# Prompt rows before the weights, one value accumulation for four samples, and ScalarE with two pages of six key slots, in a decoder step

## The reference

```python
z = x @ w_in                                   # q | k | v | B | C | h
page_sum = jnp.sum(cache_k[layer_idx, page_table], axis=2)   # block means -> top-3 blocks per head
s = einsum(q, k) / 8 - slopes * dist;  p = softmax(s where valid)
attn = einsum(p, v)
mix = concat([attn, B * causal_dwconv(C * h)]) @ w_out
x1 = layer_norm(ALPHA * x + mix)
up = causal_dwconv(x1 @ w_up);  a, g = split(up)
y = layer_norm(ALPHA * x1 + (silu(a) * g) @ w_down)
```

## Time and profile before

| | us |
|---|---|
| median of 3 runs (lowest, highest) | 438.06 (437.49, 438.96) |
| the profiled execution, own time | 437.8 |
| its span, first to last instruction | 436.0 |

### The profile page before, as it was taken

How to read it: one execution, slowest core, us unless ns; L and a number is a source line. 1 busy time by engine, 2 the same in 40 slices (tenths; PEclk the granted TensorE clock), 3 DMA queues, 4 the chain that set the end, 5 groups by cost and what they waited for, 6 DMA issues and landing times.

```text
span 436.0 us, 8237 instructions
## 1 busy us (share of the span) xinstructions
PE 412.7 (95%) x2903; PEld 339.2 (78%) x2903; DVE 294.7 (68%) x382; ACT 181.4 (42%) x694; POOL 110.8 (25%) x133
## 2 busy tenths in 40 slices
PE   4999999999999998999999989999999999999990
PEld 4588887876876774765653479999999999999990
DVE  0498999999799976954541275666776776534437
ACT  1587569644469133112110243554455555233201
POOL 1005334995255152200000717122211220000002
PEclk9999999999999999999999999999999999999997
DMA  8999999899999999999999953665556766676002
GB/s 313 397 359 407 405 407 393 316 404 409 409 359 327 338 404 405 406 405 404 402 405 398 318 196 98 194 191 162 158 169 191 213 181 186 183 211 206 3 2 99
DMA packets 109515, 124.60 MB, mean 286 GB/s; under 512 B 5903, under 2 KB 67048, under 8 KB 109466
## 3 DMA queue, kind: packets, MB, share of 16 engines
q1 hardware_dynamic: 101138, 107.30, 70.2%
q10 hardware_dynamic: 8336, 16.78, 10.2%
HBM read 121.65 MB, written 2.61 MB: 285 GB/s over the span
## 4 chain that ended last, share of the span: by engine, by line
PE 64%; DVE 18%; DMA 5%; issue 5%; SPq 4%; POOL 2%; ACT 1%; DVEq 0%; POOLq 0%; ACTq 0%
PE ps L1821 12%; PE ps L1822 11%; PE ps L1823 11%; PE ps L1714 8%; PE ps L1608 6%; DVE qk L939 6%; DVE T L949 5%; PE ps L1437 4%; PE ps L1632 4%; PE ps L1634 3%; PE ps L1384 3%; SPq L360 2%; DMA wring<-in_cache_v 2%; DMA KV<-in_cache_k 2%; POOL x1l L612 1%
## 5 line engine op out<-in xcount | busy, mean ns | idle before, releaser
L1188 DVE TENSOR_TENSOR wlo<-KV,whi 128x2048 fp32r<-128x2048 f32 (+1 forms) x24 | 61.7, 2571 | 57.5 <-ACT whi L838 29.3
L1437 PE MATMUL ps<-xT,wring 128*128 128x264 f32 x384 | 89.6, 388 | 0.1
L1437 PEld LDWEIGHTS ps<-xT,wring 128*128 128x128 f32 x384 | 71.6, 190 | 13.6 <-issue 1.7
L1821 PE MATMUL ps<-x1h,whi 128*128 128x264 f32 x256 | 73.7, 288 | 0.2
L1822 PE MATMUL ps<-x1l,whi 128*128 128x264 f32 x256 | 72.7, 284 | 0.0
L1823 PE MATMUL ps<-x1h,wlo 128*128 128x264 f32 x256 | 72.6, 284 | 0.0
L939 DVE TENSOR_TENSOR qk<-KV,qk 128x1536 f32<-128x1536 f32 (+1 forms) x32 | 67.0, 2097 | 6.6 <-DMA KV<-in_cache_k 2.7
L669 ACT ACTIVATE qk<-qk 128x64 f32<-128x64 f32 x216 | 51.9, 245 | 29.1 <-POOL qk L560 23.1
L949 DVE TENSOR_REDUCE T<-qk 128x24 f32<-128x1536 f32 (+1 forms) x32 | 58.4, 1827 | 0.0
L1821 PE MATMUL ps<-fh,whi 128*128 128x264 f32 x176 | 50.4, 286 | 0.1
L1822 PE MATMUL ps<-fl,whi 128*128 128x264 f32 x176 | 50.0, 284 | 0.0
(11 more groups left out here) (215 smaller groups left out, 574.0 us busy)
## 6 DMA issues: line engine op xcount, KB each, us to landing
KV<-in_cache_k SPq DMA_DIRECT2D x128, 256.0 KB, 6.2
KV<-in_w_ffn_up SPq DMA_DIRECT2D x32, 512.0 KB, 4.7
KV<-in_cache_v SPq DMA_DIRECT2D x60, 256.0 KB, 7.3
wring<-in_cache_v SPq DMA_DIRECT2D x56, 256.0 KB, 6.4
KV<-in_w_ffn_down SPq DMA_DIRECT2D x8, 1408.0 KB, 6.3
wring<-in_w_in ACTq DMA_DIRECT2D x5, 2048.0 KB, 14.0
zbuf<-in_cache_v SPq DMA_DIRECT2D x12, 256.0 KB, 5.3
zbuf<-in_w_ffn_up SPq DMA_DIRECT2D x3, 1024.0 KB, 10.2
```

The source lines that it names most:

```text
L1188: nc.vector.tensor_tensor(wlo[s][:, 0:n], w2[s][:, 0:n], whi[s][:, 0:n], ALU.subtract).then_inc(s_lo, 1)
L1437: ins = nc.tensor.matmul(ps[:, z_bank(n), 0:R], tile[k], xT[:, k, :], start=k == 0, stop=k == KT - 1)
L1821: nc.tensor.matmul(out, wh[k], xh[k], start=k == 0, stop=False)
```

## The change

**Start.** The prompt rows go to ACT's queue as its first transfer. The first block of `w_in` goes to SP's queue, behind a wait for `ident`, and ahead of the keys. PE's warming products use `ones` in place of `ident`, stand first in its list and number 11. Six of the eight row transposes stand before the q product, two behind it; ACT copies all eight before the first q copy. **Keys.** In the six slots of `HALVED` ACT sums two pages and DVE two; `multiply` two slots later waits for ACT's sums. **Values.** The weights of four samples lie in four buffers (two of them in `ftmp` and in `ct`/`dist`, zeroed by POOL between its key pages), each in its own eight columns, and 16 value slots accumulate in one bank. So `masked_values`, `sample_outputs` and `sample_columns` run twice and not eight times; four products with a new 4-column constant `group` replace the transposes and the sum; `sample_columns` adds the own values itself. The wait of `gate_sums(1)` for the first column goes.

```diff
+HALVED = (17, 19, 22, 24, 26, 28)
-WARM = 14
+WARM = 11
@@ SP's queue
-            sp.dma_start(rows, x_prompt[0].rearrange("(r p) d -> p r d", p=P)).then_inc(s_x, 16)
+            sp.wait_ge(s_id, 16)
+            sp.dma_start(wring[:, 0, :].rearrange("p (k n) -> p k n", k=KT),
+                         win[:, :, Z_ORDER[0] * DA:(Z_ORDER[0] + 1) * DA]).then_inc(s_win[0], 16)
             sp.wait_ge(s_pt, 16)
@@ POOL
+            nc.gpsimd.memset(ones, 1.0).then_inc(s_ones, 1)
             nc.gpsimd.memset(xsP, 0.0).then_inc(s_pad, 1)
-            nc.gpsimd.memset(ones, 1.0).then_inc(s_ones, 1)
...
+            multiply_page(23)
+            multiply_page(24)
+            pool.wait_ge(s_ho, 6)
+            nc.gpsimd.memset(Pw2, 0.0).then_inc(s_zero, 1)
+            pool.wait_ge(s_scm, 8)
+            nc.gpsimd.memset(Pw3, 0.0).then_inc(s_zero, 1)
@@ ACT, sum_products(j)
-                if j in POOLED:
-                    act.wait_ge(s_kpool, pool_pages(j + 1))
-                else:
-                    act.wait_ge(s_kused, j + 1)
-                for h in range(NH):
-                    x = prod[:, j % 2, GD * DA + h * DH:GD * DA + (h + 1) * DH]
-                    ins = nc.scalar.activation(x, x, ACT.Copy, accum_out=...)
+                for g in range(2 if j in HALVED else GD, GP):
+                    if g == GD and j in POOLED:
+                        act.wait_ge(s_kpool, pool_pages(j + 1))
+                    else:
+                        act.wait_ge(s_kused, j + 1)
+                    for h in range(NH):
+                        x = prod[:, j % 2, g * DA + h * DH:g * DA + (h + 1) * DH]
+                        ins = nc.scalar.activation(x, x, ACT.Copy, accum_out=...)
@@ ACT
-            load_win(0)
+            act.dma_start(rows, x_prompt[0].rearrange("(r p) d -> p r d", p=P)).then_inc(s_x, 16)
-            for k in range(6):
+            for k in range(KT):
                 x_copy(k)
             query(0)
-            x_copy(6)
-            x_copy(7)
             load_win(1)
@@ DVE
-                    if j not in POOLED:
+                    if j not in POOLED or j - 2 in HALVED:
                         dve.wait_ge(s_reda, act_sums(j - 1))
...
-                n = GP if j in WHOLE else GD
+                n = GP if j in WHOLE else 2 if j in HALVED else GD
...
             def sample_weights(b):
-                if b == 0:
-                    dve.wait_ge(s_zero, 2)
-                nc.vector.tensor_tensor(Pw[:, b % 2, :, 0:NH], ...
+                if b < 4:
+                    dve.wait_ge(s_zero, 2 if b < 2 else 4)
+                else:
+                    dve.wait_ge(s_vused, SLOTS * (b - 4) + SLOTS)
+                i = b % 4
+                nc.vector.tensor_tensor(weights[i][:, :, i * NH:(i + 1) * NH], ...
...
+            def sample_columns(x):
+                dve.wait_ge(s_ot, x + 1)
+                four = slice(4 * x, 4 * x + 4)
+                nc.vector.tensor_tensor(xsP[:, 0:4, four], ps[:, 5 - x, 0:16].rearrange("p (t b) -> p t b", t=4),
+                                        ownp[:, :, four], ALU.add).then_inc(s_otc, 1)
@@ PE
+            pe.wait_ge(s_ones, 1)
+            for i in range(WARM):
+                nc.tensor.matmul(ps[:, 5, 0:P], ones, ones, start=True, stop=True)
             pe.wait_ge(s_id, 16)
             pe.wait_ge(s_xs, 16)
...
-            for k in range(4):
+            for k in range(6):
                 x_transposes(k)
...
             def values(b, s):
-                    if b >= 2:
-                        pe.wait_ge(s_om, b - 1)
-                    else:
-                        pe.wait_ge(s_ht, 8)
+                    pe.wait_ge(s_ht, 8)
...
-                    ins = nc.tensor.matmul(ps[32 * g:32 * g + 32, 6 + b % 2, :], Pw[:, b % 2, GP * s + g, :], home[:, g, :],
-                                           start=s == 0, stop=s == SLOTS - 1)
+                    ins = nc.tensor.matmul(ps[32 * g:32 * g + 32, 6 + b // 4, :], weights[b % 4][:, GP * s + g, :], home[:, g, :],
+                                           start=v % 16 == 0, stop=v % 16 == 15)
...
             def sample_outputs(x):
                 pe.wait_ge(s_om, x + 1)
+                pe.wait_ge(s_soft, 2)
                 for t in range(4):
-                    ins = turn(ps[:, out_bank(b), t * P:(t + 1) * P], OM[:, b % 2, t * P:(t + 1) * P])
+                    ins = nc.tensor.matmul(ps[:, 5 - x, 4 * t:4 * t + 4], OM[:, x, t * P:(t + 1) * P], group, start=True, stop=True)
```

More of the change, by code:

```diff
@@ L201, in build @@
         hT = [hT0, hT1]
+        weights = [Pw[:, 0], Pw[:, 1], Pw2, Pw3]
         rT = xT
@@ L592, in _ @@
             multiply_page(22)
-            for j in range(23, 30):
+            multiply_page(23)
[4 more added lines that the diff above has]
+            nc.gpsimd.memset(Pw3, 0.0).then_inc(s_zero, 1)
+            for j in range(25, 30):
                 multiply_page(j)
@@ L1390, in _ @@
             ins.then_inc(s_xsps, 1)
-            for i in range(WARM):
-                nc.tensor.matmul(ps[:, 5, 0:P], ident, ident, start=True, stop=True)
             def x_transposes(k):
@@ L1410, in _ @@
             ins.then_inc(s_qsps, 1)
-            for k in range(4, 6):
+            for k in range(6, KT):
                 x_transposes(k)
@@ L1545, in _ @@
             z_tile(7)
[L1546 removed]
+            pe.wait_ge(s_const, 16 * 9)
             pe.wait_ge(s_qb, NS)
@@ L1745, in _ @@
             early_half(1, 1)
-            value_range(17, 19)
-            value_range(19, 20)
-            sample_outputs(2)
+            value_range(17, 20)
+            sample_outputs(0)
             value_range(20, 21)
```

91 lines of the change are left out of this document (27 added, 64 removed).

## The result

The changed kernel takes 444.64 us (median of 4, 443.86 to 445.26) against 437.84 (4 runs, 437.49 to 438.96): ratio 1.0150, interval 1.0127 to 1.0172. The change makes the kernel slower by 6.8 us. The forecast was 438.6 with a range of 436.2 to 440.3, so it is wrong, and by more than any of its rivals allowed. The profiled execution took 443.86 us with a span of 442.1.

A forecast was written before the change was run, and what follows sets the result against it. Early supply of loads through three gates was taken as the bound, DMA near 405 GB/s. 437.8 + 0 (start) + 0.65 (slot 19) - 0.1 (end) = 438.35; median 0.26 above: 438.6 us. Range 436.2 to 440.3, own range 437.4 to 439.4.

The forecast's parts named there:

- Three gates in a row: Keys landed at 33.8 us, penalties at 99.67, value product 1 at 136; time gained only between gates is lost.
- Start at zero: New start gains 0 at the end, bounds -0.6 to +0.7; bytes ahead of sample 1's keys fix their landing.
- Rival (c): Weight block 3, asked for earlier, delays key slots needed at 38 and 42 us: 0.7 to 1.5 us slower; chance 0.16.
- The gain at the start itself: Before the first gate: q product and DVE's first key product about 1.9 us earlier, first projection tile some 2.9.
- rival (e): Rows land no sooner or PE transposes at the lower clock; first gate hides it, time unchanged; chance 0.52 with the forecast.
- PE's 2.9 us of lead: PE's 2.9 us gained at the start are lost at `gate_sums(0)`, which waits for reduction 15.
- Slot 19 at +0.65: ACT's eight extra sums delay tile 22's copy and value slot 0 (126.80 to about 127.45): cost 0.65 us, bounds 0 and 1.91.
- Rival (d): PE, idle longer before the late values, falls to 1.2 GHz; some 3 us reach the end, 441.6 us; chance 0.06.
- Rival (b): The 2.00 us issue of value slot 4's load at the third gate moves into a wait: 1.67 us less, 436.9; chance 0.08.
- Values at nothing: PE loses 28 of 32 transposes, gets four more short products; no term in the sum.
- the other halved slots: Slots 17, 22, 24, 26, 28: ACT's extra sums fit into waits or free time, DVE's savings don't show; no term.
- The end at -0.1: After the last value slot, the smaller column sum is covered by a weight load: -0.1 us, bounds 0 and -0.9.

The follow-up runs named there:

- test with the later request: Kernel before with the new start, second weight block requested behind query 1 (439.46 us, ratio 1.0042) or behind the sums of slot 0 (440.65 us, 1.0058).
- keys first: Kernel before with the new start, first key slot of sample 1 issued ahead of the eight constants: 439.34 us, ratio 1.0036.
- filled wait: Kernel before with the new start, three unused matmuls in PE's wait at 65 to 68 us: 438.48 us, ratio 1.0024.

## Why the prediction was wrong, point by point

- **Three gates in a row** held in the main. Product 4, the penalties and value slot 1 all moved, and the shift at the third gate is that of the end but for SP's issue. But the third gate lets lateness through unequally: 1.2 us cost nothing in the shared accumulation alone, and 7.76 us cost 6.1.
- **Start at zero** failed: 2.1 us. That the time of issue does not decide at the first gate is right (4 us of earlier issue brought 0.55). But I took the bytes that pass by 32.5 us as given by the earlier trace rows, and in the changed kernel they were fewer: 11.30 MB instead of 11.76 by 33 us, so +1.2 instead of 0, outside the bounds of -0.6 to +0.7. Part of it may go with the ninth constant, which the sum left out: the shared accumulation alone, with the old start, has 11.62 MB. The 1.3 us from the last byte to the landing, used in this sum, stand in no row. Rival (c) had the sign right and its kind of cause, keys that land behind DVE's work, but at 38 and 42 us instead of at 35; that the block asked for earlier is what holds them back, the test with the later request did not show.
- **The gain at the start itself**, 1.9 us for DVE's first product, came in one of the eleven traces with the new start (keys first, 16.08 us); the others have 17.31 to 18.06. In these ten the q product took 2.62 to 3.64 us instead of 1.92, in spite of the products on ones. In nine of them the granted clock reads 0.50 to 0.56 in a window of 2 us between 8 and 18 us. The changed kernel's own trace reads 1.00 there, but its row transposes take 0.69 instead of 0.44 us, as in the new start alone where the clock reads 0.50, and its q product 2.95. That is rival (e), and as it says, the gate hides it: product 4 waits 3.04 us all the same. The q product of the changed kernel, and DVE at the gate:

```profile
11.85 2.95 PE L1407 MATMUL ps<-wring,xsP 128*32 128x512 f32 x16
...
35.08 2.29 DVE L948 TENSOR_TENSOR qk<-KV,qk 128x2048 f32<-128x2048 f32 x1 [3.04 <-DMA KV<-in_cache_k]
```

- **PE's 2.9 us of lead "go at `gate_sums(0)`"** failed. They went earlier, in a wait of 3.1 us from 65 to 68 us for ACT's copy of k and v rows, and the granted clock fell behind it. By the filled wait this costs 1.3 us of the median; in the traces most of it comes through the collision of POOL with product 18.
- **Slot 19 at +0.65, bounds 0 to 1.91** is the step that failed most: 4.6 to 4.8. I followed the copy of tile 22 along ACT and PE, and wrote that POOL's last gating would end at "the same place". It ends at 132.7. POOL needs tile 22 (its third gating), then page 21, then the fourth gating, in that order, so the full 1.91 passes to POOL; and two of its steps now fall beside DVE's products (2.13 instead of 0.73, 1.76 instead of 0.25 us), while the fourth gating no longer does (0.72 instead of 1.40). With the old start, slot 0 comes 3.4 us late, of which the denominators have 0.4. Of the 4.6 us the lower clock behind the wait is 1.9.
- **Rival (d), the clock,** was the right mechanism in the wrong place: I looked at 225 to 240 us, where nothing happened, and gave it 0.06. I had asked where PE would be idle longer only for the part of the change that takes work from PE, not for the parts that delay others or send PE ahead. The Trainium skill, "TensorE: Matmul & The Clock Gate", section "HAM oscillation — how this bites in real kernels", says that waits for loads between short bursts let the clock fall back and each burst starts at half rate. The traces agree on the fall to half rate; here the waits were for ACT and for POOL, and a wait of 3.1 us brought the fall in some executions and not in others.
- **Rival (b), SP's long issue,** came true (1.88 instead of 3.54 us), and hid 1.66 us of the loss. It is no luck of one kernel: in the other 16 traces, too, these issues took less than before, 1.88 to 3.32 us. But how much less does not follow from the lateness alone (1.88 us when 0.6 late, 2.78 when 5.0 late), and what sets it is open.
- **Values at nothing** held (ratio 1.0002), though the prediction miscounts PE's part: 8 short products replace all 32 transposes. So did **the other halved slots** (without slot 19 the change stands where the new start alone stands, 439.84 and 439.79). **The end at -0.1** can't be told apart.
- **The forecast's own range** of 437.4 to 439.4 does not follow from the bounds of its three terms: added up on 438.6 they give 436.6 to 440.7. The measured time lies outside either.
- **"What would show it"**: the q product at 11.85 is near the 11.4 given, the first tile at 16.97 already 1.1 behind the 15.9; 33.89 moved by 1.19 and 99.67 by 2.25, where 0.6 was the bound, and slot 0 by 6.1 where 0.6 was said.

## What to carry to other kernels

When work is moved to an engine that looks idle, list every engine that waits for the next copy behind it, and follow each list separately up to the gate: here the third engine in the row, POOL, was the late one, and moving one call ahead of the sums was worth 3.2 us. For each wait of TensorE that a change makes longer, in any part of the program, add the price of the lower clock, or put unused matmuls there; it made half of this loss. And don't carry a sum of bytes over to a new order of transfers: here 0.46 MB less had passed by the gate.

## What I had not expected of the hardware

- **POOL's multiplies and DVE's products shut each other out.** A POOL multiply of 32 columns that takes 0.25 us beside a DVE reduction takes 1.76 when it starts 0.1 us behind a DVE product; DVE's product of 1.75 us takes 2.83 when POOL's pages are under way. The one that comes second ends late by about what is left of the first: in the new start alone POOL's pages end at 105.67, DVE began at 104.44, and its product took 1.1 us longer. The Trainium skill, "SBUF — State Buffer", section "Who interferes with whom", states this as an exclusive lock on a shared port pair; the traces agree. A shift of 1.5 us of POOL's work decided whether 1.1 us was paid.
- **The granted clock fell behind single waits of 2.2 and 3.1 us in a full program**, though not in every execution, and stayed down for 3 to 4 us: value slot 0 took 1.93 instead of 1.07 us, and the eight matmuls behind it 2.81 instead of 2.05.
- **DMA engines that are busy all the time moved 299 to 402 GB/s** within the same kernel, in stretches that differ in what was in flight.
- **Issuing one DMA instruction took 2.00 us** The earlier trace rows where its like takes 0.33, and in the changed kernel, which reaches the place 7.8 us later, all four issues took 1.88 us together. SP's list alone does not say which instruction it will be.
